# A hybrid encoder block: square root and reciprocal replaced by Ln, Exp and multiplications, head and seam rearranged, another order at the entry of the large product

## The reference

```python
xn = rms_norm(x, norm_mix_g); z = xn @ w_in            # columns: [B | C | h | q | k | v], 512 each
u = C * h; y_conv = B * (conv3(u) + conv_b)            # causal, 3 taps, per channel
q, k = rms_norm(q, q_gain), rms_norm(k, k_gain)        # 8 heads of 64
scores = q @ k_band.T * 64**-0.5 + bias                # 9 chunks of 64 keys
y_attn = softmax(scores) @ v_band
y_mix = concat(group_rms_norm(y_conv, g, 64), group_rms_norm(y_attn, g, 64))
h   = x + y_mix @ w_out
out = h + square(relu(rms_norm(h, norm_mlp_g) @ w_mlp_in)) @ w_mlp_out     # D_FF 4096
```

## Time and profile before

| | us |
|---|---|
| median of 3 runs (1193.72, 1195.67, 1195.95) | 1195.67 |
| the profiled execution | 1192.94 |
| its span, first to last instruction | 1191.0 |
| PE busy | 1131.7 |
| DVE busy | 762.8 |
| POOL busy | 629.2 |
| ACT busy | 533.7 |

### The profile page before, as it was taken

One profiled execution on the slowest core, in us unless ns is written; L12 is line 12 of the kernel. 1 busy time (PEld: TensorE's weight loads), 2 busy tenths in 40 slices (PEclk: granted clock), 3 DMA queues, 4 the chain that ended last, 5 costly groups with the idle time before them and its releaser, 6 DMA issues.

```text
span 1191.0 us, 14699 instructions
## 1 busy us (share of the span) xinstructions
PE 1131.7 (95%) x5368; PEld 938.1 (79%) x5368; DVE 762.8 (64%) x860; ACT 533.7 (45%) x835; POOL 629.2 (53%) x349
## 2 busy tenths in 40 slices
PE   4999999999999989998799999999998999999998
PEld 4778878877887877787688888888877888888887
DVE  7567867876786787444343443435358677776788
ACT  5454454455446464313445444454544333343331
POOL 3421240322124012035668888878769699696892
PEclk9999999999999999899999999999999999999999
DMA  7210110111010142220245444444487635445324
GB/s 230 92 53 18 50 49 11 53 37 35 18 51 22 50 167 90 102 72 36 62 141 195 141 165 145 159 159 142 136 287 267 211 106 170 151 134 197 110 87 159
DMA packets 98512, 135.81 MB, mean 114 GB/s; under 512 B 8072, under 2 KB 52112, under 8 KB 98456
## 3 DMA queue, kind: packets, MB, share of 16 engines
q1 hardware_dynamic: 95104, 131.13, 32.9%
q10 hardware_dynamic: 3352, 3.94, 1.1%
HBM read 97.27 MB, written 39.34 MB: 115 GB/s over the span
## 4 chain that ended last, share of the span: by engine, by line
PE 79%; issue 8%; DVE 5%; POOL 3%; ACT 2%; DMA 1%; SPq 0%; DVEq 0%; POOLq 0%; ACTq 0%
PE PJ L1473 15%; PE SC L1727 9%; PE PJ L1727 9%; PE OS L1727 7%; PE PJ L1764 6%; PE PT L1764 6%; PE SC L1764 6%; PE OS L1764 6%; PE PJ L1549 5%; PE SC L1507 3%; PE OS L1531 2%; PE PT L1518 1%; POOL wsl L506 1%; DVE sq L1016 1%; POOL wsl L504 1%
## 5 line engine op out<-in xcount | busy, mean ns | idle before, releaser
L1473 PE MATMUL PJ<-actT,wsl 128*128 128x512 f32 (+1 forms) x1176 | 299.8, 398 | 2.4 <-POOL wsl L506 2.4
L1473 PEld LDWEIGHTS PJ<-actT,wsl 128*128 128x128 f32 x1176 | 211.8, 192 | 40.8 <-POOL wsl L506 2.8
L616 POOL TENSOR_TENSOR ring<-b,ring 128x1024 fp32r<-128x1024 f32 x48 | 137.8, 2879 | 37.8 <-ACT ring L944 37.6
L1382 DVE TENSOR_TENSOR ring<-hraw,ring 128x1024 fp32r<-128x1024 f32 x56 | 151.3, 2738 | 3.8 <-ACT ring L939 3.8
L504 POOL CAST wsl<-raw 128x1024 fp32r<-128x1024 f32 x24 | 26.9, 1121 | 199.6 <-PE PJ L1473 183.9
L939 ACT ACTIVATE ring<-hraw 128x1024 fp32r<-128x1024 f32 x56 | 59.2, 1058 | 134.4 <-PE OS L1764 62.6
L1727 PE MATMUL OS<-actT,w1a 128*128 128x512 f32 x384 | 93.4, 391 | 1.7 <-ACT p1s L880 1.7
L723 ACT ACTIVATE prob<-prob,negm 128x640 f32<-128x640 f32 (+4 forms) x64 | 44.6, 697 | 107.9 <-DVE negm L1090 107.7
L1764 PE MATMUL PJ<-ring 128*128 128x512 f32 x336 | 82.2, 395 | 6.1 <-POOL ring L616 4.5
L1016 DVE RECIPROCAL sq<-sq 128x256 f32<-128x256 f32 (+1 forms) x43 | 82.5, 1925 | 3.9 <-ACT sq L690 3.9
L1727 PEld LDWEIGHTS OS<-actT,w1a 128*128 128x128 f32 x384 | 71.6, 188 | 16.5 <-POOL w1a L557 1.9
(11 more groups left out here) (193 smaller groups left out, 2227.7 us busy)
## 6 DMA issues: line engine op xcount, KB each, us to landing
hraw<-hidd SPq DMA_DIRECT2D x56, 512.0 KB, 3.6
w1r<-in_w_mlp_in SPq DMA_DIRECT2D x16, 1024.0 KB, 6.1
hidd<-hs SPq DMA_DIRECT2D x64, 256.0 KB, 2.0
b<-in_w_mlp_out SPq DMA_DIRECT2D x16, 1024.0 KB, 6.5
raw<-in_w_in SPq DMA_DIRECT2D x24, 512.0 KB, 3.7
hidd<-h SPq DMA_DIRECT2D x48, 256.0 KB, 2.3
xin<-in_x SPq DMA_DIRECT2D x8, 512.0 KB, 8.5
woraw<-in_w_out SPq DMA_DIRECT2D x8, 512.0 KB, 7.5
```

What stands on the lines that cost most here:

```text
L616: nc.gpsimd.tensor_tensor(duo(n)[1][LO], W2_SRC[name][:, 2 * d:2 * d + 2], duo(n)[1][HI].bitcast(F32), ALU.subtract).then_inc(s["wl2_done" ...
L1382: vec.tensor_tensor(duo(n)[0][LO], hraw[:, n % HRING], duo(n)[0][HI].bitcast(F32), ALU.subtract).then_inc(s["hl2_done"], 1)
L1473: last = mm(PJ[:, g % 2, cols], wsl[:, w % NSLOT, a, k], actT[:, b, k, c], start=(r == 0), stop=(r == 3 * KD - 1))
```

## The change

**Norms.** `deviation` is now Ln of the sum, Exp of it times -0.5 (that is r, the inverse root as ACT gives it), and a Square of r into a new tile `rt`; `inverse` is one Newton step in two SCALAR_TENSOR_TENSORs on DVE, the first of which reads SS. `ss_read` is counted by that first one. `o_dev` and `o_norm` change alike, on 128x8 values. The sign of the step is taken up by a factor -1 on the convolution's gain.

**Moves in the attention.** `sum_squares` 2 and 3 go from 1b and 3b to 2a and 4a; deviation 2 from unit 1 to unit 2, ahead of `take(3)`; deviation 3 from unit 3 to 4; DVE's steps follow. The copy of the pair's parameters (`prm`) goes from the seam to 2b.

**Head.** DVE scales and subtracts in another order; POOL splits the second weights only when four tiles are scaled, and its memset of qz stands behind the third weights; the transposes 4 to 7 go to groups 1 and 2; ACT's `take` and deviation stand among `x_hi`.

**Entry of the large product.** W1_PREP is gone, all engines follow W1_ORDER, in which P3 and P4 of piece 0 stand ahead of P6, P7 and P5 of piece 1. PE places the units between thirds of a product; two DVE sums move behind a unit; POOL forms six of its sums earlier.

```diff
-W1_ORDER = (W1_HEAD + [("P6", 1), ("P3", 0), ("P7", 1), ("P4", 0), ("P5", 1)]
+W1_ORDER = (W1_HEAD + [("P3", 0), ("P4", 0), ("P6", 1), ("P7", 1), ("P5", 1)]
...
-W1_PREP = W1_HEAD + [("P3", 0), ("P4", 0), ("P6", 1), ("P5", 1), ("P7", 1)] + W1_ORDER[12:]
...
+                    if w == 1 and first:
+                        pool.wait_ge(s["xs_done"], 4)
...
+                    if w == 2 and first:
+                        pool.wait_ge(s["tr_done"], NT)
+                        pool.wait_ge(s["w_ready"], 3)
+                        for slot in QZ:
+                            nc.gpsimd.memset(qz[HEADS[0], :, slot, :].bitcast(F32), 0.0).then_inc(s["qz_zero"], 1)
+                        pool.wait_ge(s["qz_zero"], len(QZ))
...
-                act.activation(sq[:, zbuf(n)], SS[:, :], ACT.Sqrt, bias=eps[:, 0:1], scale=1.0 / HD).then_inc(s["ss_read"], 1)
+                act.activation(sq[:, zbuf(n)], SS[:, :], ACT.Ln, bias=eps[:, 0:1], scale=1.0 / HD).then_inc(s["dev_done"], 1)
+                act.wait_ge(s["dev_done"], it * 18 + 3 * n + 1)
+                act.activation(sq[:, zbuf(n)], sq[:, zbuf(n)], ACT.Exp, scale=-0.5).then_inc(s["dev_done"], 1)
+                act.wait_ge(s["dev_done"], it * 18 + 3 * n + 2)
+                act.activation(rt[:, n % 2], sq[:, zbuf(n)], ACT.Square, scale=(0.5 / HD) ** 0.5
+                               ).then_inc(s["dev_done"], 1)
...
-                    if u == 1:
+                    if u == 2:
                         deviation(it, 2)
-                    if u == 2:
                         take(it, 3)
                     if u == 3:
+                        v_copy(it, 1)
+                    if u == 4:
                         qk_hi(it, 2)
-                        v_copy(it, 1)
                         deviation(it, 3)
-                    if u == 4:
+                    if u == 5:
                         v_hi(it, 1)
-                    if u == 5:
+                        c_copy(it, 0)
                         qk_hi(it, 3)
-                        c_copy(it, 0)
...
-            x_hi(NT - 2)
-            x_hi(NT - 1)
+            x_hi(4)
+            x_hi(5)
+            take(0, 1)
+            x_hi(6)
             deviation(0, 0)
-            take(0, 1)
+            x_hi(7)
             deviation(0, 1)
...
+                r0, w = sq[:, zbuf(n)], rt[:, n % 2]
                 if part != 1:
+                    dve.wait_ge(s["dev_done"], it * 18 + 3 * n + 3)
+                    vec.scalar_tensor_tensor(w, SS[:, :], HD * EPS, w, ALU.add, ALU.mult).then_inc(s["ss_read"], 1)
+                if part != 0:
                     dve.wait_ge(s["ss_read"], it * 8 + (TURN[n] + 3 + extra))
-                op = vec.reciprocal(sq[:, b, c], sq[:, b, c])
-                if part != 0:
-                    op.then_inc(s["rs_done" if n < 4 else "rsc_done"], 1)
+                    vec.scalar_tensor_tensor(r0, w, 1.5, r0, ALU.subtract, ALU.mult).then_inc(s["rs_done" if n < 4 else "rsc_done"], 1)
...
-                    if at == "1b":
+                    if at == "2a":
                         sum_squares(it, 2)
-                    if at == "3b":
+                    if at == "4a":
                         sum_squares(it, 3)
...
-            for n, u in ((1, 7), (2, 9), (3, 11)):
-                unit_transpose(u)
-                product(n, range(6))
-                unit_transpose(u + 1)
-                product(n, range(6, 12))
+            unit_transpose(7)
+            product(1)
+            unit_transpose(8)
+            product(2, range(4))
+            unit_transpose(9)
+            product(2, range(4, 8))
...
```

More of the change, by code:

```diff
@@ L571, in t1234 @@
                 nc.gpsimd.tensor_tensor(xb, xb, yb, ALU.subtract).then_inc(s["tt_done"], 1)
-            for n, (name, i) in enumerate(W1_PREP):
+            for n, (name, i) in enumerate(W1_ORDER):
                 if n < 3:
@@ L580, in _ @@
                     w1_sum(0, 1)
-                if name == "P6" and i:
+                if name == "P6" and i >= 2:
                     w1_sum(i, 0)
                     w1_sum(i, 1)
-                if name == "P7":
+                if name == "P7" and i >= 2:
                     w1_sum(i, 2)
                 w1_lo(n)
-                if name == ("P7" if i < 2 else "P5"):
+                if name == "P5" and i >= 2:
                     w1_sum(i, 3)
+                if (name, i) == ("P6", 0):
+                    w1_sum(0, 2)
+                    w1_sum(0, 3)
+                if (name, i) == ("P5", 0):
+                    w1_sum(1, 0)
+                    w1_sum(1, 1)
+                if (name, i) == ("P4", 0):
+                    w1_sum(1, 2)
+                    w1_sum(1, 3)
             def w2_sum(b, j, d):
@@ L732, in o_dev @@
                 act.wait_ge(s["oss_done"], it * 2 + (g + 1))
-                act.activation(osd[:, :], oss[:, :], ACT.Sqrt, bias=eps[:, 0:1], scale=1.0 / HD).then_inc(s["osd_done"], 1)
+                act.activation(osd[:, :], oss[:, :], ACT.Ln, bias=eps[:, 0:1], scale=1.0 / HD).then_inc(s["osd_done"], 1)
+                act.wait_ge(s["osd_done"], it * 4 + (2 * g + 1))
+                act.activation(osd[:, :], osd[:, :], ACT.Exp, scale=-0.5).then_inc(s["osd_done"], 1)
             def o_store(it, g):
@@ L861, in w1_hi @@
             def w1_hi(n):
[L862 removed]
+                name, i = W1_ORDER[n]
                 if name in ("P1", "P2", "P4"):
@@ L998, in _, with x_lo @@
             dve.wait_ge(s["g_in"], 16)
-            for t in range(NT):
+            def x_lo(t):
+                dve.wait_ge(s["xhi_done"], t + 1)
+                lo_part(t, slice(t * P, (t + 1) * P))
+            for t in range(3):
                 x_scale(t)
-                if t >= 2:
-                    dve.wait_ge(s["xhi_done"], t - 1)
-                    lo_part(t - 2, slice((t - 2) * P, (t - 1) * P))
+            x_lo(0)
+            x_scale(3)
+            for t in range(1, 4):
+                x_lo(t)
+            for t in range(4, NT):
+                x_scale(t)
             def squares_lo(it, n):
@@ L1213, in extras, with prepare @@
                     inverse(it, 5, 1)
-            def iteration(it, last):
+            def prepare(it):
                 dve.wait_ge(s["ss_read"], it * 8 + 4)
@@ L1219, in iteration @@
                 vec.memset(ub[:, 0:2], 0.0).then_inc(s["halo_done"], 1)
+            def iteration(it, last):
                 dve.wait_ge(s["bias_in"], it * 64 + 64)
@@ L1259, in _ @@
             squares_lo(0, 0)
-            for t in (NT - 2, NT - 1):
-                dve.wait_ge(s["xhi_done"], t + 1)
-                lo_part(t, slice(t * P, (t + 1) * P))
+            for t in range(4, NT):
+                x_lo(t)
             dve.wait_ge(s["prm_in"], 16 * 10)
@@ L1350, in _ @@
                     unit_lo(t - 1)
-            t13(3)
             for n in range(7, len(UNITS_T)):
@@ L1354, in _ @@
                 if n == 7:
+                    t13(3)
+                if n == 8:
                     t24(3, 0)
```

104 lines of the change are left out of this document (54 added, 50 removed).

## The result

The changed kernel takes 1205.71 us in the median (1204.29 to 1207.12), the kernel before on the same chip 1194.7: a ratio of 1.0093 (95% interval 1.0074 to 1.0112), 11 us slower. The sign and the range (1200 to 1238) held; the forecast of +24 was more than twice too large.

What follows compares the result with a forecast made beforehand. PE, busy 1131.7 of 1191.0 us, was taken as the bound, so its waits and clock counted. Terms summed to +23.6 on 1192.94, giving 1216.6, and 2.7 more for the median: 1219 us (8 in 10: 1200 to 1238).

Steps and rivals of the forecast that it cites:

- seams, pairs, parameter copy: Attention: +4.7 per seam (+14.2), later deviations inside iterations +12.7, parameter copy moved out of the seam -1.8 us.
- head: Start to first score: deviations and DVE's multiplications delay the first score from 54.47 to 57.6 us, +3.1.
- attention's end: Wait of 2.7 at k = 3 comes; the 2.77 on the gain vector and its low clock go: -3.5 us.
- entry: Entry of the large product: waits on ymix, p1s and w1a and a low clock shrink or go, -9.6 us.
- clock in the pairs: Attention part: twelve waits over 1.8 us instead of six, seven low-clock stretches for two, +8.5 us.
- ahead of group 6: Inside an iteration, unit 2: deviation 2 ahead of take(3) makes PE wait 3.1 us.
- seven or more windows: Sign to look for in the profile after: seven or more half-speed windows before the output product.
- step 3 of the seam: Seam: bias DMAs, q halves, deviation 1 and vT copy delay the transposes of v from 152.57 to 156.9, +4.4 us.
- (B): Rival: no loads between Ln and Exp, so seams and head cost nothing; 1167 us, chance 0.05.
- (C): Rival: the links of a seam hide in each other and only the first lasts; 1188.5 us, chance 0.11.
- (D): Rival: DVE's new operations wait for POOL, which also brings low clock; +17, 1234 us, chance 0.16.
- (E): Rival: the entry of the large product gives back half, POOL's early sums being the bound; 1224 us, chance 0.06.

Runs made afterwards that it cites:

- experiment 1: The kernel before with only the new entry of the large product: 1186.3 us (0.9922); the changed kernel with the old entry: 1216.0 us (1.0179).
- experiment 2: The changed kernel with one line more, loading one table set that holds both Ln and Exp: 1166.0 us (0.9754).
- experiment 5: The changed kernel with take(1) ahead of deviation(0) where one pair turns into the next: 1224.9 us (1.0242).
- experiment 7: New functions, deviations 2 and 3 in the old places, with none, one, two loads per deviation: 1173.0, 1178.3, 1190.4 us; moved places: 1166.0, 1177.4, 1205.7.
- experiment 3: The kernel of experiment 2 with a load put back between each Ln and its Exp: 1177.4 us (0.9853).

## Why the prediction was off

Its steps against what was measured (the two profiled pairs, before to after, and the experiments):

| step | forecast | measured |
|---|---|---|
| seams, pairs, parameter copy | +25.1 | +21.6 (stretches taken off) |
| head | +3.1 | +0.3, -1.3 |
| attention's end | -3.5 | -1.7, -0.1 |
| entry | -9.6 | -9.8, -11.3; -9.3 and -10.3 alone |
| clock in the pairs (forecast: with the head) | +8.5 | +1.4, +0.6; three executions against three 0 |
| second product | 0 | +0.6, -0.2 |
| sum | +23.6 | +12.3, +9.3; medians +11 |

**The mechanism was right.** The loads stand before each Ln and each Exp; ACT's queue, not its mean load (50%), makes PE wait. The waits came where they were worked out: ahead of group 6 (forecast 3.1, measured 2.99), ahead of the scores of unit 8 (2.3, 2.06), in the seam (1.8 and 1.60), in the head (3.6 by position, 3.63 measured) and at k = 3 (2.7, 2.51). The head's 3.6 is in part luck: PE is there at 41.8 and not at 44.0, the operand at 45.4 and not at 47.6, and only their distance was right. The entry was right to 0.2 in the pair of traces, and experiment 1 shows it as a term of its own.

**The step that failed is the clock term, +8.5.** From one execution of the kernel before I counted two stretches for six waits of about 2 us, and I priced the changed kernel at seven stretches for twelve waits, each at 1.7 us. Measured ahead of the output product were four and five in the changed kernel, and five in experiment 1's kernel with the new attention part, for two, five and five with the old one; up to the first `w1a` product sixteen and sixteen. So the term is about 0. The sign that I had named, seven or more windows, did not come.

The mean granted clock, which is on record for every run, says the same. Of 47 runs of the kernel before, 25 have 0.989 or more, like the profiled one (0.991), and the others 0.985 to 0.988; the changed kernel has 0.989 to 0.991 in all of its five. Worked out as twice the missing share of the clock times the span, this is some 28 us at half speed in the mean of the kernel before and 27 in the five runs of the changed kernel with the old entry: no more.

Three errors in the count can be named. The base of two was from one of the executions with few. It left out the kernel before's wait in the head (2.43), while the twelve have the head's. And waits of 1.6 to 1.8 us, as in the seam, and a length of 3 us for 2 were priced as if they brought more. In all fourteen profiled executions together, from the first full clock to the first `w1a` product, half speed followed none of 88 waits of 0.5 to 1.5 us, one of 47 of 1.5 to 1.9, 35 of 66 of 1.9 to 2.5, and 26 of 39 of 2.5 and more (it began between the start of the wait and 2 us after its end).

The number of long waits alone does not give the stretches either. The kernel before has 8 of 1.9 us and more up to the first `w1a` product, the changed one 11, and in three executions each 15 of 24 and 14 of 33 were followed. Why the three more cost nothing stays open. Nor is the clock nothing in general: with nearly all long waits gone (experiment 2) no stretch is left, and with the seam's wait at 4.14 (experiment 5) there are twelve.

**The head** was mis-sized by 2.8 and 4.4 us. PE after and before, at the start:

```profile
20.79 7.84 PE L1512 MATMUL PJ<-actT,wsl 128*128 128x256 f32 x52
...
45.41 0.47 PE L1525 MATMUL OS<-sqh,ones 128*128 128x512 f32 x1 [3.63 <-DVE rt L1045]
...
51.28 0.66 PE L1608 MATMUL PT<-ident,vT 128*128 128x128 f32 x4
...
54.77 0.44 PE L1546 MATMUL SC<-kT,qT 128*128 128x128 f32 x3
```

```profile
22.63 2.91 PE L1473 MATMUL PJ<-actT,wsl 128*128 128x256 f32 x12
```

The first block of products starts 1.8 us earlier and runs on for 7.8 us where it was broken off after 2.9 for a block of transposes, and the trace grants full clock from 22.9 us on, not 27.0 (executions with the new head 20.1 to 22.9, three with the old head 25.5 to 27.0). I had moved single steps only and kept the old clock. And the transposes of v at 51.28 did not wait, since PE stood behind anyway by its 3.63: two lateness terms that I had added hide in each other.

**Pairs and seams**: 25.1 forecast, 21.6 measured (pair by pair, without the stretches: 6.9, 6.2, 5.0, 3.5). A seam costs 4.3 and not 4.7; inside pair 1 PE's waits rise from 3.2 to 5.3 us, +2.1 and not +3.4, since the small waits that I had added beside the two large ones (0.6 at unit 12 and others) did not appear; the last pair costs 3.5, not 2.5. (In step 3 of the seam the terms as given add up to 156.9, not to 156.3, so that the sum would have been 5.3 a seam.)

**Attention's end**: the 2.77 on the gain vector went, the 2.51 on `wo` came, and the clock that I had counted as saved is again one that comes and goes (two and one stretches before, one and one after). Without it the step is about 0.

**The rivals.** (B) Wrong for this program, whose trace shows the loads; but its price, 1167, is what experiment 2 gives (1166.0) once the loads are gone. That they meet so closely is in part luck: the head fell by 2.9 us where (B) had 0, and attention's end by 3.5 where it had 6.2. The Trainium skill (ScalarE: Activation LUTs, Table sets: the hidden batching unit) counts one load for ln then exp. Here 24 loads stand before the Ln and 24 before the Exp, and what the page says came true only when its set was loaded by name. This case's trace does not agree with it for a program that names none. (C) Links of a chain hiding in each other: so in the head, not in the seam. (D) Denied: the second multiplication takes 0.72. (Its price as given, 1234, is that of the profiled execution; on the median it would be 1236.) (E) Denied by experiment 1.

The 11 us are thus, by the ratios of the experiments: the entry -9.3; the new functions with their loads, seams, head and end +3.6 (0.9952 against 0.9922); the moved places +16.8 (1.0093 against 0.9952). Why the move was worth making without loads and harmful with them is the table of experiment 7.

## What to carry to other kernels

Before a function is exchanged on ACT, read in the program's order which table loads it brings, and ask whether one set holds both functions: one line here turned +11 us into -29. The place of a long operation in a queue is good or bad only for one length of it: look for idle time just ahead of it (it should move there) and for who stands behind it. And price clock losses from several executions, or from the mean granted clock of all runs on both sides, never from the stretches of one trace.

## What the runs showed of the hardware

The granted clock differs between executions of one program whose waits agree to 0.1 us: 13.6 and 20.5 us at half speed up to the first `w1a` product of the kernel before. In the fourteen profiled executions a wait of 1.9 us or more was followed by a half-speed stretch in 61 of 105 cases, one of 1.5 to 1.9 in one of 47, and one of 0.5 to 1.5 in none of 88. A table load costs 1.283 us in every group, also when the set that it loads is already there (experiment 3), and where the activation behind it waits for nothing else it starts 0.01 to 0.02 us later.
